# Seven of eight 128-row tiles of a second layer's input transposed by VectorE in 32x32 blocks and by SBUF-to-SBUF transfers

## Chip, cores, metric

One Trainium2 chip, one of its cores. The metric is the device time of one launch in microseconds (us); lower is better.

## What is computed

A two-layer decoder trunk over 1024 prompt tokens and 32 sample tokens, with 1024 features, all float32. Layer 0 mixes tokens with a gated short convolution, layer 1 with a gated linear recurrence (HGRN2). Both layers have this shape:

```
h = rms_norm(x, norm_pre[i])
proj = h @ w_in[i]                      # 1024 x 4096
o = mixer(proj)                         # convolution or recurrence, gated by silu(z)
x = x + rms_norm(o @ w_out[i], norm_post[i])
```

The change touches the place between the layers: layer 0's last line, and layer 1's first (`x` after layer 0, normalised by its rows, and brought from rows of tokens to columns of tokens, since the projection contracts over features and needs features on the partitions).

## The kernel before

Everything is written by hand, engine by engine, with counted semaphores; an engine runs its instructions in the order in which they are written. The token rows of the prompt are cut into eight tiles of 128 (below "row 0" to "row 7"; index `i`, `CK` = 8). Matrix products are made with a high and a low part of each float32 operand, as three products.

The stage between the layers runs like this, for each row i:

- **TensorE** makes the output product of the row (`products`, 48 matmuls of 128x512, L819) into two PSUM banks, 2(i mod 3) and the next. Rows 0 to 2 are done together, first; rows 3 to 7 follow one by one, and row i starts only when VectorE has read row i-3 out of those banks (event `t1`). The transposes of a finished row stand within the products of a later row (`TURN`): `turn_rows(i)` is eight 128x128 transposes against the identity (L836) into banks 6 and 7.
- **ScalarE** squares the product for the norm (`squares_y`, L1390), takes the root (L1397), squares the new x (L1390 again), takes its root, makes the high part of the transposed previous row (`turned_hi`, L1423), and starts the squares of the next row.
- **VectorE** scales the product by `norm_post` (L2082), adds the residual (L2092, event `x1`), scales the previous row's transpose by `norm_pre` out of PSUM (`turned`, L2107), normalises its own row (L2140, event `xn`), and makes the low part of the previous row's transpose (`turned_lo`, L2113).
- **SP** issues the transfers: the new x of the row to DRAM (L494), and the load of x for row i+3 (`load_x`, L456), which waits for `xn` of row i and for the store to have landed, since both use the same one of three buffers.

The normalised row is in `o_n[i % 2]` (its first use in row i is as scratch of ScalarE's squares), its transpose in `o_tr[i % 2]`. The 32 sample tokens have a path of their own; their transpose lies in `o_tr[1]` until its low half is made (event `lo` of `Q_DVE[0]`, L2072), after row 0's low half.

After row 7's product TensorE goes on to layer 1: groups of 24 matmuls (L674), one for a third c of the tokens (352 columns) and a projection i. Their order is `FIRST`, and row 7's transposes stand behind the second group:

```
FIRST = ((0, 0), (0, 1), (1, 0), (1, 1), (0, 2), (1, 2), (2, 0), (2, 1), (2, 2))
pe.wait_ge(V_TR.sem, V_TR.at((2, 5, 7)[c], "lo"))       # first projection alone
```

So group (0, 0) needs rows 0 to 2 transposed and split, group (0, 1) rows up to 5, group (0, 2) all of them. Group (1, 0) writes the bank of group (0, 0), which ScalarE empties (L1438) behind the high half of row 6. In row 6 (`CK - 2`) ScalarE and VectorE also split two weight tiles for layer 1 (L1184, L1715).

Of the kernel before, what the change touches and what calls it, by code (L numbers as in the profile page):

```python
# [41 lines left out]
F_FLOOR = 2.061153622438558e-09  # L42
QSCALE = float(P) ** -0.5
B4, B8 = 4, 8
NG = 4
GR = NSAMP // NG
LEVELS = (8, 16, 32, 64)
# [45 lines left out]
def build(nc, x_prompt, x_sample, state_conv, state_hgrn, norm_pre, w_in, conv_w, lb_logits, onorm,  # L93
          w_out, norm_post, y_prompt, y_sample, conv_p, conv_s, hgrn_p, hgrn_s):
    ctx = ExitStack()
    with ctx:
# [3 lines left out]
        def sem(name):  # L100
            return ctx.enter_context(nc.semaphore(name))
# [210 lines left out]
        A_P2 = Events(sem("out2_act"), ["s0", "s1", "sd1"])  # L312
        V_P2 = Events(sem("out2_dve"), ["t0", "ms", "t1", "rs", "x"])
        first_half_x = sem("first_half_x")
        Q_PE = [Events(sem("sample_pe"), ["y", "n1", "n2", "tr"]), Events(sem("sample2_pe"), ["y", "n1"])]
        Q_ACT = [Events(sem("sample_act"), ["sq", "sd", "sq2", "sd2", "hi"]), Events(sem("sample2_act"), ["sq", "sd"])]
        Q_DVE = [Events(sem("sample_dve"), ["t", "rs", "x", "rs2", "xn", "g", "lo"]),
# [42 lines left out]
        def wsrc(w, col):  # L360
            return w[:, bass.ds(col, P)].rearrange("(k p) c -> p k c", p=P)
# [34 lines left out]
        def _(sp):  # L396
# [81 lines left out]
            sp.wait_ge(cout, 32)  # L478
            sp.dma_start(o_g, norm_post[0:1, :].broadcast_to([P, D])).then_inc(g_in, 16)

            QC, FC, VC, ZC = 0, D, 2 * D, 3 * D
            for i in range(CK):
                if i == 0:
                    for first in range(3):
                        load_x(first)
                    sp.wait_ge(Q_PE[0].sem, Q_PE[0].at(0, "y"))
                    load_w(NW2, wsrc(w_in[1], VC), 0, None)
                    load_w(NW2 + 1, wsrc(w_in[1], QC), 1, None)
                    sp.wait_ge(Q_DVE[0].sem, Q_DVE[0].at(0, "x"))
                    for q in range(4):  # L490
                        cols, own = quarter(q)
                        sp.dma_start(x1_dram[NP:T, cols], smp_x[0][own, :]).then_inc(smp_kept, 16)
                sp.wait_ge(V_PO.sem, V_PO.at(i, "x1"))
                sp.dma_start(x1_dram[i * P:i * P + rows_of(i), :], o_x[i % 3][0:rows_of(i), :]).then_inc(stored[i % 3], 16)  # L494
                if i + 3 < CK:
                    load_x(i + 3)
            load_w(NW2 + 2, wsrc(w_in[1], FC), 0, None)
            with sp.Fori(1, KT) as j:
                for t, col in enumerate((QC, ZC - P, VC, FC)):
# [131 lines left out]
        def _(pe):  # L631
# [193 lines left out]
            def turn_rows(i):  # L825

                r = rows_of(i)
                pe.wait_ge(V_PO.sem, V_PO.at(i, "xn"))
                if i == 0:
                    pe.wait_ge(Q_DVE[0].sem, Q_DVE[0].at(0, "g"))  # L830
                if i:
                    pe.wait_ge(V_TR.sem, V_TR.at(i - 1, "gb"))
                for half, name in enumerate(("ta", "tb")):
                    for k in range(4):
                        kk = half * 4 + k
                        mm = nc.tensor.transpose(bank[6 + half][:, k * P:k * P + r],  # L836
                                                 o_n[i % 2][0:r, kk * P:(kk + 1) * P], ident[0:r, 0:r])
                    mm.then_inc(P_TR.now(name), 1)
# [35 lines left out]
            for cc in range(2):  # L874
                mm = nc.tensor.transpose(bank[7][:, (1 + cc) * P:(2 + cc) * P], smp_n[:, cc * P:(cc + 1) * P], ident[:, :])
            mm.then_inc(Q_PE[0].now("tr"), 1)
            TURN = {(3, 3): 0, (4, 3): 1, (4, 7): 2, (5, 7): 3, (6, 3): 4, (6, 7): 5, (7, 7): 6}
            for i in range(3, CK):
                pe.wait_ge(V_PO.sem, V_PO.at(i - 3, "t1"))
                for k in range(KT):  # L880
                    b = 2 * (i % 3)
                    mm = products(k, ((b, 0), (b + 1, 1)), wout_tile(reg_b, k), o0, i, k == 0, k == KT - 1)
                    if k == KT - 1:
                        mm.then_inc(y_done, 1)
                    elif i == CK - 1 and k < 2:
                        mm.then_inc(w_used, 1)
                    if (i, k) in TURN:
                        turn_rows(TURN[i, k])


            h1, o1 = planes(reg_a), planes(reg_b)
# [284 lines left out]
        def _(act):  # L1176
# [233 lines left out]
            def squares_y(i):  # L1410

                r = rows_of(i)
                if i >= 2:
                    act.wait_ge(P_TR.sem, P_TR.at(i - 2, "tb"))
                act.wait_ge(y_done, i + 1)
                for half in range(2):
                    square(bank[2 * (i % 3) + half][0:r, :], o_n[i % 2][:, half * HALF:(half + 1) * HALF], A_PO,
# [290 lines left out]
        def _(dve):  # L1708
# [386 lines left out]
            def turned(i):  # L2095

                r = rows_of(i)
                dst = o_tr[i % 2].rearrange("p (k t) -> p k t", k=KT)
                if i >= 2:
                    dve.wait_ge(A_TR.sem, A_TR.at(i - 2, "hi"))  # L2100
                    dve.wait_ge(V_TR.sem, V_TR.at(i - 2, "lo"))
                for half, (name, g_name) in enumerate((("ta", "ga"), ("tb", "gb"))):
                    dve.wait_ge(P_TR.sem, P_TR.at(i, name))
                    src = bank[6 + half][:, :].rearrange("p (k t) -> p k t", k=4)[:, :, 0:r]
                    first = PRE + KT + 4 * half
                    g = cst[:, first:first + 4].unsqueeze(2).broadcast_to([P, 4, r])
# [15 lines left out]
            for i in range(CK):  # L2122
# [9 lines left out]
                    sample_next("xn")  # L2132
                elif i == 1:
                    sample_next("g")
                if i:
                    turned(i - 1)
                dve.wait_ge(A_PO.sem, A_PO.at(i, "sd2"))
                V.reciprocal(col(i, "rs2", r), col(i, "sd2", r)).then_inc(V_PO.now("rs2"), 1)
                dve.wait_ge(V_PO.sem, V_PO.at(i, "rs2"))
                V.tensor_scalar(o_n[i % 2][0:r, :], o_x[i % 3][0:r, :], col(i, "rs2", r), None,  # L2140
                                ALU.mult).then_inc(V_PO.now("xn"), 1)
                if i:
                    turned_lo(i - 1)
                if i == 1:
                    sample_next("lo")
# [373 lines left out]
```

## Time and profile before

| | |
|---|---|
| time, median of 3 runs | 1034.37 us (1034.27 to 1034.69) |
| span of the profiled execution | 1032.7 us |
| TensorE busy | 1025.7 us, 99% of the span |
| VectorE busy | 705.2 us, 68% |
| ScalarE busy | 426.3 us, 41% |
| matmuls of layer 0's output product (L819, rows 0 to 7) | about 353 to 453 us |
| row 7's transposes on TensorE | from 460.9 us |

The span runs from the first to the last instruction; the time of a launch is 1.7 us more. Busy times are sums over the whole kernel, so what counts for the change is the stage from about 385 to 475 us from the span's start.

### The profile page before, as it was taken

The numbers are of one execution on the slowest core, as the hardware profiler recorded it, in microseconds if no ns is written. First come the engines' busy times: TensorE is split into PE (matmuls) and PEld (weight loads), VectorE is DVE, ScalarE is ACT, GpSimd is POOL, SyncE is SP. The second block draws the span as 40 slices with busy tenths as digits, with TensorE's granted clock in tenths as the row PEclk, the third lists the DMA queues.
The fourth block names the chain that finished last, engine by engine and source line by source line (L and its number), as shares of the span: only waits on it lengthen the run. The fifth ranks groups of instructions, "written<-read, shape, count | busy, mean of one in ns | idle before, by whom it ended". The sixth has DMA issues, their size and how long they took to land.

```text
span 1032.7 us, 20543 instructions
## 1 busy us (share of the span) xinstructions
PE 1025.7 (99%) x7979; PEld 977.3 (95%) x7979; DVE 705.2 (68%) x1274; ACT 426.3 (41%) x860; POOL 18.3 (2%) x45
## 2 busy tenths in 40 slices
PE   9999999999999999999999999999999999999998
PEld 8999999999999978899999999999999999997886
DVE  6899677677776926762857768485776848586355
ACT  7444333333333624443345443443534344383222
POOL 2000000000000000000000000000000000000000
PEclk9999999999999999999999999999999999999999
DMA  8003121112112253321212211221221122143064
GB/s 253 22 22 82 42 82 41 41 53 69 41 41 63 101 173 114 120 82 42 58 46 64 63 35 49 63 59 45 61 61 43 41 63 61 60 150 110 25 241 169
DMA packets 95552, 78.75 MB, mean 76 GB/s; under 512 B 2965, under 2 KB 86886, under 8 KB 95510
## 3 DMA queue, kind: packets, MB, share of 16 engines
q1 hardware_dynamic: 77622, 69.19, 21.5%
q10 hardware_dynamic: 17888, 8.98, 3.0%
q8 instruction: 29, 0.48, 0.2%
q14 instruction: 13, 0.11, 0.0%
HBM read 64.72 MB, written 13.44 MB: 76 GB/s over the span
## 4 chain that ended last, share of the span: by engine, by line
PE 97%; DVE 2%; DMA 1%; ACT 0%; SPq 0%; issue 0%; DVEq 0%
PE bank L674 36%; PE bank L731 28%; PE bank L819 14%; PE bank L699 4%; PE bank L1069 4%; PE bank L913 2%; PE bank L1025 1%; PE bank L1018 1%; PE bank L1027 1%; PE bank L929 1%; PE bank L801 1%; PE bank L921 1%; PE bank L836 1%; PE bank L1013 1%; PE bank L977 1%; PE bank L908 1%
## 5 line engine op out<-in xcount | busy, mean ns | idle before, releaser
L674 PE MATMUL bank<-reg_a,wsplit 128*128 128x352 f32 x2304 | 381.5, 324 | 0.0
L674 PEld LDWEIGHTS bank<-reg_a,wsplit 128*128 128x128 f32 x2304 | 368.6, 188 | 1.1
L731 PE MATMUL bank<-reg_a,wsplit 128*128 128x264 f32 x1344 | 165.7, 284 | 0.0
L731 PEld LDWEIGHTS bank<-reg_a,wsplit 128*128 128x128 f32 x1344 | 164.1, 188 | 0.2 <-DVE arena L1902 0.2
L731 PE MATMUL bank<-reg_b,w_ring 128*128 128x264 f32 x1008 | 124.6, 284 | 0.0
L731 PEld LDWEIGHTS bank<-reg_b,w_ring 128*128 128x128 f32 x1008 | 123.3, 188 | 0.0
L819 PE MATMUL bank<-reg_b,reg_a 128*128 128x512 f32 x288 | 69.3, 396 | 0.0
L819 PEld LDWEIGHTS bank<-reg_b,reg_a 128*128 128x128 f32 x288 | 53.7, 188 | 12.7 <-issue 0.4
L1930 DVE TENSOR_TENSOR arena<-arena,bank 128x264 f32<-128x264 f32 x84 | 34.8, 427 | 34.2 <-PE bank L731 33.1
L1290 ACT ACTIVATE arena<-bank 128x264 f32<-128x264 f32 x84 | 32.3, 390 | 55.1 <-PE bank L731 50.4
L1268 ACT ACTIVATE w_ring<-wraw 128x512 fp32r<-128x512 f32 x42 | 26.1, 632 | 69.1 <-PE bank L731 69.0
L2413 DVE COPY arena<-bank 128x128 f32<-128x128 f32 x8 | 2.3, 292 | 66.2 <-PE bank L1018 66.2
L1268 ACT ACTIVATE wsplit<-wraw 128x512 fp32r<-128x512 f32 x42 | 25.0, 628 | 49.1 <-DMA wraw<-in_w_in 36.1
L1715 DVE TENSOR_TENSOR wsplit<-wraw,wsplit 128x1024 fp32r<-128x1024 f32 x32 | 39.1, 1222 | 4.7 <-ACT wsplit L1184 4.7
L819 PE MATMUL bank<-reg_a,reg_b 128*128 128x512 f32 x168 | 39.8, 394 | 0.0
L2441 DVE SCALAR_TENSOR_TENSOR arena<-arena,bank 128x352 f32<-128x352 f32 x45 | 23.3, 518 | 24.0 <-ACT arena L1434 18.6
L819 PEld LDWEIGHTS bank<-reg_a,reg_b 128*128 128x128 f32 x168 | 31.6, 188 | 7.5
L1184 ACT ACTIVATE wsplit<-wraw 128x1024 fp32r<-128x1024 f32 x32 | 33.7, 1054 | 0.7 <-PE bank L819 0.7
L1440 ACT ACTIVATE arena<-bank 128x352 f32<-128x352 f32 x24 | 11.2, 465 | 55.1 <-PE bank L674 55.0
L2082 DVE TENSOR_TENSOR arena<-bank,arena 128x512 f32<-128x512 f32 x24 | 16.3, 686 | 25.1 <-ACT arena L1390 25.0
L1878 DVE TENSOR_TENSOR w_ring<-wraw,w_ring 128x512 fp32r<-128x512 f32 x42 | 28.8, 690 | 6.5 <-ACT w_ring L1268 6.5
L1492 ACT ACTIVATE kv_stacked<-v_stacked,bmask 96x128 fp32r<-96x128 f32 x64 | 19.6, 391 | 31.6 <-DVE arena L2349 31.6
(299 smaller groups left out, 1499.5 us busy)
## 6 DMA issues: line engine op xcount, KB each, us to landing
wraw<-in_w_in SPq DMA_DIRECT2D x64, 512.0 KB, 4.1
first_x<-in_x_prompt SPq DMA_DIRECT2D x8, 512.0 KB, 7.4
wraw<-in_w_out SPq DMA_DIRECT2D x8, 512.0 KB, 4.0
w_out_raw<-in_w_out SPq DMA_DIRECT2D x8, 512.0 KB, 5.1
arena<-in_w_out SPq DMA_DIRECT2D x8, 512.0 KB, 4.7
arena<-in_x_prompt SPq DMA_DIRECT2D x8, 512.0 KB, 3.3
x_scratch<-arena SPq DMA_DIRECT2D x8, 512.0 KB, 2.6
arena<-in_state_hgrn ACTq DMA_DIRECT2D x8, 512.0 KB, 3.8
```

What stands on the lines that cost most here:

```text
L674: mm = nc.tensor.matmul(bank[b][:, 0:CH], w[wi][:, k, :], rhs[hi], start=(k == 0 and i == 0), stop=(k == KT - 1 and i == 2))
L699: mm = nc.tensor.matmul(bank[b][:, 0:QT], w[wi][:, k, :], src[hi][:, k % KH, cols], start=(k == 0 and i == 0), stop=(k == KT - 1 and i == 2))
L731: mm = nc.tensor.matmul(bank[banks[q]][:, 0:QT], w[wi][:, k, :], B_OP[name][hi][:, k, q * QT:(q + 1) * QT], start=(start and k == 0 and i ...
L819: mm = nc.tensor.matmul(bank[b][0:r, :], src[side][:, k, i * P:i * P + r], w[wi][:, half * HALF:(half + 1) * HALF], start=(start and side ...
L1069: mm = nc.tensor.matmul(bank[PART_BANK[n]][:, :], o1[side][:, k, i * P:(i + 1) * P], wout_tile(reg_a, k)[wi][:, half * HALF:(half + 1) * H ...
L1184: A(wsplit[:, s, 0] if dst is None else dst, wraw[:, s], ACT.Copy).then_inc(w_hi, 1)
L1268: A(w_block(name)[0], A_RAW[name], ACT.Copy).then_inc(W_HI.now(name), 1)
L1290: A(dst[:, q * QT:(q + 1) * QT], bank[banks[q]][:, 0:QT], ACT.Copy).then_inc(C_ACT.now(f"{what}{s}{q}"), 1)
L1715: V.tensor_tensor(d, wraw[:, s], h.bitcast(F32), ALU.subtract).then_inc(w_lo, 1)
L1878: V.tensor_tensor(lo, A_RAW[name], hi.bitcast(F32), ALU.subtract).then_inc(W_LO.now(name), 1)
L1930: V.tensor_tensor(dst[:, cols], src[:, cols], bank[banks[q]][:, 0:QT], ALU.add).then_inc(C_DVE.now(f"{what}{s}{q}"), 1)
L2441: V.scalar_tensor_tensor(buf[:, cols], buf[:, cols], QSCALE if kind == "q" else 1.0, bank[c][:, 0:CH], ALU.mult, ALU.mult).then_inc(bank_f ...
```

## The change

Rows 0 to 6 are no longer transposed by TensorE. VectorE transposes the 32x32 blocks of the normalised row in place (`V.transpose`), and SP then moves each block row into its place with 16 transfers of 32 partitions, 8 feature tiles and 32 elements (32 KB each, runs of 128 bytes). VectorE then scales the transpose by `norm_pre` in one instruction in SBUF. The old buffers' waits become waits for the transfers. Row 7 and the sample tokens are transposed as before. `turned(i - 1)` has also moved on VectorE from ahead of row i's normalisation to behind it.

```diff
+            def move_row(i):
+
+                sp.wait_ge(row_turned, i + 1)
+                if i == 1:
+                    sp.wait_ge(Q_DVE[0].sem, Q_DVE[0].at(0, "lo"))
+                elif i >= 2:
+                    sp.wait_ge(V_TR.sem, V_TR.at(i - 2, "lo"))
+                blocks = o_n[i % 2].rearrange("p (k d t) -> p d k t", k=KT, d=NQD)
+                rows = o_tr[i % 2].rearrange("p (k b t) -> p b k t", k=KT, b=NQD)
+                for d in range(NQD):
+                    for b in range(NQD):
+                        sp.dma_start(rows[d * BLK:(d + 1) * BLK, b],
+                                     blocks[b * BLK:(b + 1) * BLK, d]).then_inc(row_moved[i % 2], 16)
...
                 if i + 3 < CK:
                     load_x(i + 3)
+                if i < LAST_ROW:
+                    move_row(i)
...
-            TURN = {(3, 3): 0, (4, 3): 1, (4, 7): 2, (5, 7): 3, (6, 3): 4, (6, 7): 5, (7, 7): 6}
...
-                    if (i, k) in TURN:
-                        turn_rows(TURN[i, k])
...
                 if i >= 2:
-                    act.wait_ge(P_TR.sem, P_TR.at(i - 2, "tb"))
+                    act.wait_ge(row_moved[i % 2], i // 2 * MOVED)
...
+                if i < LAST_ROW:
+                    dve.wait_ge(row_moved[i % 2], (i // 2 + 1) * MOVED)
+                    g = cst[:, PRE + KT:PRE + 2 * KT].unsqueeze(2).broadcast_to([P, KT, r])
+                    V.tensor_tensor(dst, dst, g, ALU.mult).then_inc(*V_TR.many("ga", "gb"))
+                    return
...
-                if i:
-                    turned(i - 1)
                 dve.wait_ge(A_PO.sem, A_PO.at(i, "sd2"))
                 V.reciprocal(col(i, "rs2", r), col(i, "sd2", r)).then_inc(V_PO.now("rs2"), 1)
                 dve.wait_ge(V_PO.sem, V_PO.at(i, "rs2"))
                 V.tensor_scalar(o_n[i % 2][0:r, :], o_x[i % 3][0:r, :], col(i, "rs2", r), None,
                                 ALU.mult).then_inc(V_PO.now("xn"), 1)
+                if i < LAST_ROW:
+                    dve.wait_ge(V_PO.sem, V_PO.at(i, "xn"))
+                    V.transpose(o_n[i % 2], o_n[i % 2]).then_inc(row_turned, 1)
                 if i:
+                    turned(i - 1)
                     turned_lo(i - 1)
```

On VectorE, one row of the loop (row 2) stood like this before, from the scaling of the product to the low part of row 1 (L2082 scales the product, L2107 the transpose, L2140 normalises, L2113 makes the low part):

```order
L2082 TENSOR_TENSOR arena<-bank,arena 128x512
L2085 RECIPROCAL small<-small 128x1
L2092 SCALAR_TENSOR_TENSOR arena<-arena,small 128x1024
L2107 TENSOR_TENSOR arena<-bank,cst 128x512 x2
L2138 RECIPROCAL small<-small 128x1
L2140 TENSOR_SCALAR arena<-arena,small 128x1024
L2113 TENSOR_TENSOR reg_a<-arena,reg_a 128x8x128
```

And so after the change, where the lines are some 16 to 20 higher (L2098 for L2082, L2118 for the scaling of the transpose, L2158 for L2140, L2133 for L2113, and L2162 is new):

```order
L2098 TENSOR_TENSOR arena<-bank,arena 128x512
L2101 RECIPROCAL small<-small 128x1
L2108 SCALAR_TENSOR_TENSOR arena<-arena,small 128x1024
L2156 RECIPROCAL small<-small 128x1
L2158 TENSOR_SCALAR arena<-arena,small 128x1024
L2162 STREAM_TRANSPOSE arena<-arena 128x1024
L2118 TENSOR_TENSOR arena<-arena,cst 128x1024
L2133 TENSOR_TENSOR reg_a<-arena,reg_a 128x8x128
```

The scaling of the previous row's transpose has moved from between the residual and the normalisation to behind the new block transpose, directly ahead of the low part.

On SP's queue, rows 0 to 2 are now written like this (L514 is the store that was L494, L462 the load that was L456, L498 the new transfers; `arena` holds `o_x`, `o_n` and `o_tr` alike):

```order
L514 DMA x_scratch<-arena 128x1024
L462 DMA arena<-in_x_prompt 128x1024
L498 DMA arena<-arena 32x8x32 x16
L514 DMA x_scratch<-arena 128x1024
L462 DMA arena<-in_x_prompt 128x1024
L498 DMA arena<-arena 32x8x32 x16
```

The 16 transfers of a row stand behind that row's store and load and ahead of the next row's; rows 5 and 6 have no load. Before, the same queue held the L494 and L456 rows alone.

## Rows read from the trace of the kernel before

**Rows 1.** The page: span, TensorE's line, and its granted clock in tenths.
```profile
span 1032.7 us, 20543 instructions
...
PEclk9999999999999999999999999999999999999999
```

**Rows 2.** Chain that ended last, 380 to 475 us: start, duration, piece.
```profile
391.57 5.58 PE bank L819 x24
397.15 0.87 PE bank L836 x8
398.02 11.17 PE bank L819 x48
...
453.52 7.69 PE bank L674 x48
```

**Rows 3.** Waits, 382 to 475 us: total, times, longest.
```profile
DVE arena L2107 <- PE bank L836: 16.3, 6, 5.7
```

**Rows 4.** Timeline, ScalarE and VectorE, one row of tokens: start, duration, instruction, idle before.
```profile
409.67 1.29 DVE L2107 TENSOR_TENSOR arena<-bank,cst 128x512 f32<-128x512 f32 x2 [5.41 <-PE bank L836]
...
410.99 1.06 ACT L1423 ACTIVATE reg_a<-arena 128x1024 fp32r<-128x1024 f32 x1 [5.22 <-DVE arena L2107]
...
414.69 1.28 DVE L2092 SCALAR_TENSOR_TENSOR arena<-arena,small 128x1024 f32<-128x1024 f32 x1
...
416.01 1.06 ACT L1390 ACTIVATE arena<-arena 128x1024 f32<-128x1024 f32 x1 [1.69 <-DVE arena L2092]
...
417.72 0.75 DVE L2140 TENSOR_SCALAR arena<-arena,small 128x1024 f32<-128x1024 f32 x1
```

**Rows 5.** VectorE groups by shape, whole kernel: busy us, mean ns.
```profile
L2206 DVE COPY_PREDICATED arena<-mask_within,bank 64x512 f32<-64x512 uint8 x14 | 10.4, 741 | 0.1
...
L2113 DVE TENSOR_TENSOR reg_a<-arena,reg_a 128x1024 fp32r<-128x1024 f32 x8 | 9.8, 1226 | 2.2 <-ACT reg_a L1423 2.1
...
L2140 DVE TENSOR_SCALAR arena<-arena,small 128x1024 f32<-128x1024 f32 x8 | 6.0, 754 | 0.3
```

**Rows 6.** Timeline of SP's DMA queue, 340 to 500 us.
```profile
361.77 0.43 SPq L472 DMA_DIRECT2D arena<-in_x_sample  x1
362.24 0.42 SPq L473 DMA_DIRECT2D arena<-in_norm_post  x1
...
365.49 0.76 SPq L475 DMA_DIRECT2D out<-arena  x1
...
389.23 0.34 SPq L494 DMA_DIRECT2D x_scratch<-arena  x1
392.33 0.37 SPq L456 DMA_DIRECT2D arena<-in_x_prompt  x1
```

**Rows 7.** DMA view: queues, then issues with median us to landing.
```profile
q1 hardware_dynamic: 77622, 69.19, 21.5%
q10 hardware_dynamic: 17888, 8.98, 3.0%
...
x_scratch<-arena SPq DMA_DIRECT2D x4, 32.0 KB, 1.7
```

**Rows 8.** Timeline, VectorE: first row's normalised tile; the sample tokens' lower half.
```profile
390.94 0.76 DVE L2140 TENSOR_SCALAR arena<-arena,small 128x1024 f32<-128x1024 f32 x1
...
401.19 0.42 DVE L2072 TENSOR_TENSOR reg_a<-arena,reg_a 128x256 fp32r<-128x256 f32 x1
```

**Rows 9.** Timeline, end of the stage, as rows 4.
```profile
442.95 1.28 DVE L2092 SCALAR_TENSOR_TENSOR arena<-arena,small 128x1024 f32<-128x1024 f32 x1
...
445.27 1.04 ACT L1390 ACTIVATE arena<-arena 128x1024 f32<-128x1024 f32 x1
...
458.03 0.75 DVE L2140 TENSOR_SCALAR arena<-arena,small 128x1024 f32<-128x1024 f32 x1
458.65 0.45 ACT L1438 ACTIVATE arena<-bank 128x352 f32<-128x352 f32 x1
...
461.83 8.41 PE L674 MATMUL bank<-reg_a,wsplit 128*128 128x352 f32 x51
```

More of the change, by code:

```diff
@@ L44 @@
 B4, B8 = 4, 8
+BLK = 32
+NQD = P // BLK
+MOVED = NQD * NQD * 16
+LAST_ROW = CK - 1
 NG = 4
@@ L314, in build @@
         first_half_x = sem("first_half_x")
+        row_turned = sem("rows_turned_in_blocks")
+        row_moved = [sem(f"row_blocks_moved{i}") for i in range(2)]
         Q_PE = [Events(sem("sample_pe"), ["y", "n1", "n2", "tr"]), Events(sem("sample2_pe"), ["y", "n1"])]
@@ L828, in turn_rows @@
                 pe.wait_ge(V_PO.sem, V_PO.at(i, "xn"))
-                if i == 0:
-                    pe.wait_ge(Q_DVE[0].sem, Q_DVE[0].at(0, "g"))
-                if i:
-                    pe.wait_ge(V_TR.sem, V_TR.at(i - 1, "gb"))
+                pe.wait_ge(Q_DVE[0].sem, Q_DVE[0].at(0, "g"))
                 for half, name in enumerate(("ta", "tb")):
@@ L2098, in turned @@
                 dst = o_tr[i % 2].rearrange("p (k t) -> p k t", k=KT)
-                if i >= 2:
-                    dve.wait_ge(A_TR.sem, A_TR.at(i - 2, "hi"))
-                    dve.wait_ge(V_TR.sem, V_TR.at(i - 2, "lo"))
+                if i < LAST_ROW:
[3 more added lines that the diff above has]
+                    return
+                dve.wait_ge(A_TR.sem, A_TR.at(i - 2, "hi"))
+                dve.wait_ge(V_TR.sem, V_TR.at(i - 2, "lo"))
                 for half, (name, g_name) in enumerate((("ta", "ga"), ("tb", "gb"))):
-                    dve.wait_ge(P_TR.sem, P_TR.at(i, name))
+                    dve.wait_ge(P_TR.sem, P_TR.at(0, name))
                     src = bank[6 + half][:, :].rearrange("p (k t) -> p k t", k=4)[:, :, 0:r]
@@ L2134, in _ @@
                     sample_next("g")
-                if i:
-                    turned(i - 1)
                 dve.wait_ge(A_PO.sem, A_PO.at(i, "sd2"))
```

## The prediction, made before the run

> **What bounds the kernel now.** The chain that ended last comes first: between 380 and 475 us it is TensorE alone, piece behind piece [rows 2]. A row's 48 matmuls take 11.17 us there, and the eight transposes of a row stand in it with 0.87 us. The clock is full in every slice [rows 1]. So seven transposes less are worth 7 x 0.87 = 6.1 us, the most that this change can give, as long as nobody else makes TensorE wait. The next view is who else is near. The waits show VectorE waiting 16.3 us for the transposes [rows 3]; TensorE has no wait of note. That wait goes, and something else takes its place, so the loop over VectorE, ScalarE and now SP must be costed, not only TensorE. The timeline of one row of tokens gives its pieces [rows 4]. The loop has a deadline: group (0, 1), which needs rows to 5; row 7's transposes, which need row 7 normalised; and group (1, 0), which needs ScalarE past row 6's high half. It starts at 461.83 us now [rows 9], and I take the change in that start as the change in the kernel's time, since behind it the chain is TensorE without gaps.
>
> **TensorE's side.** Row 3 starts at 391.57 us; five rows of 11.17 us end at 447.4 us, where group (0, 0) could start instead of at 453.52 us [rows 2]. That is the 6.1 us.
>
> **The loop over VectorE and ScalarE.** Call T(i) the end of row i's block transpose, M(i) the landing of its last transfer. Behind T(i), VectorE must scale row i-1's transpose, wait for ScalarE's high part, make the low part, do all of row i+1 to its normalisation, and transpose again. Before, the same pieces run from 409.67 us (scaling begins) to 417.72 + 0.75 = 418.47 us (row normalised): 8.80 us without a wait for TensorE [rows 4]. The squares and the root of the new x, from 416.01 us to just ahead of 417.72, are in it in full, so that nothing more is exposed when the scaling no longer lies beside them. The scaling becomes one SBUF instruction, 1.29 us to about 1.23 us (the 128x1024 tensor-tensor form) [rows 4, 5]: 8.74 us. The block transpose is new, and the trace shows none. Bounds: 0.75 us, the fastest 128x1024 row, and 1.48 us, twice a predicated copy of 512 elements [rows 5]. I take 1.23 us, as for other one-element-a-cycle forms of the width. So C = 10.0 us a row, of 11.17 us that TensorE needs. The slack is 1.2 us a row, if the transfers of a row land within C.
>
> **The transfers.** Sixteen issues a row on SP. The nearest issue is one of 32 partitions: 0.43 us, and 0.47 us from start to start (361.77 to 362.24) [rows 6]: 16 x 0.465 = 7.4 us. The bounds are 0.34 us (the 128-row store) and 0.76 us (the three-level store L475) [rows 6]. The last one lands 1.7 us after its issue if it is like the 32 KB store [rows 7]: 15 x 0.465 + 1.7 = 8.7 us from the row's first issue. Each of the 16 DMA engines gets 256 runs of 128 bytes a row. The ACT queue's packets took 3.0% of 16 x 1032.7 us for 17,888, that is 27.7 ns for 502 bytes; SP's took 45.8 ns for 891 bytes [rows 7]. A line through both says 4 ns and 0.046 ns a byte, 10 ns for 128 bytes; so 256 of them take between 2.7 and 7.1 us, less than their issue, but behind the 512 KB load just ahead of them in the queue. The upper value adds about 1.5 us. I take 9.6 us from first issue to landing.
>
> SP's own round also matters, and every transfer in it counts: the 16 issues (7.4), then the next row's store, whose landing the next load waits for (389.23 to 392.33 is 3.1 us from store to load), then the load's issue (0.37) [rows 6]. Before, this wait lay behind other things. Now it stands between two rows' transfers: 10.9 us, and 11.2 us with some of the queueing. Queued behind these issues on SP are also the store and load of the next rows, which have slack, and the weight load behind row 7's store.
>
> The Trainium skill bears on the packet price: DMA: Bandwidth & Descriptors, "Why small descriptors are slow (HBM only)", says that SBUF-to-SBUF transfers do not pay the small-run penalty, while its "Specifications" ask for 512 bytes for line rate. No row here has runs of 128 bytes. By the one the sum is bound by the issue, by the other it is the slow rival below.
>
> **The sum, row by row.** T(0) = 390.94 + 0.76 + 1.23 = 392.9 us [rows 8]; the first issue follows, S(0) = 392.95, M(0) = 402.55. Row 1's transfers write `o_tr[1]`, so they wait for the sample's low part, which stands behind row 0's scaling, high and low parts: 1.23 + 1.06 + 1.23 + 0.42 = 4.0 us behind M(0) [rows 4, 5, 8]. That is a wait of its own, S(1) = 406.55, M(1) = 416.15. Then S(2), S(3), S(4) = 417.75, 428.95, 440.15 (11.2 apart), M(2), M(3), M(4) = 427.35, 438.55, 449.75. The transposes: T(2) = M(0) + 10.0 + 0.4 (sample) = 412.95, and T(i) = M(i-2) + 10.0 for the next ones, since each M comes 1 to 3 us behind the T of the row after it: T(5) = 448.55. T(6) = 449.75 + 10.0 + 0.9 = 460.65 us. The 0.9 us is row 6's two weight splits on ScalarE: the square comes 1.04 us behind the residual there (end 444.23, start 445.27) [rows 9], in other rows 0.04 us (415.97, 416.01) [rows 4].
>
> From T(6) on: row 5's scaling, high and low parts, 3.6 us (464.25: group (0, 1) may start); the weight split on VectorE 1.23 us; row 7 from its scaling to its residual 2.7 us (what remains of the 8.80 us without the other pieces) and on to its normalisation 2.5 us (415.97 to 418.47) (470.7: row 7's transposes on TensorE); M(6) = T(6) + 9.6 = 470.3 is just ahead; row 6's scaling 1.23 us, high part 1.06 us, bank emptied by ScalarE 0.45 us [rows 4, 9]. Group (1, 0) starts at about 473.5 us instead of 461.83: **+11.7 us**. On the median this gives 1034.4 + 11.7 = 1046.1 us; the profiled execution's span lies 1.7 us below the median before, and I expect 1044.4 us for it. TensorE saves 6.1 us and then stands for some 18 us: before (0, 0), (0, 1), row 7's transposes and (1, 0).
>
> **The rivals.**
>
> *Cheap transfers.* If issues come 0.34 us apart, transfers land 6.8 us after the first issue and SP's round is 8.9 us, under C. Then VectorE's loop alone decides: M(0) = 399.75, T(2) = 410.15, T(6) = 451.5, (1, 0) at 464.3: +2.5 us, 1037 us. With a block transpose of 0.75 us it is 2.9 us less, 1034 us. For it: such issues are in the trace. Against it: none of them has partial partitions.
>
> *The saving shows.* The other sign: VectorE's loop keeps ahead of TensorE. With a 0.75 us transpose and transfers that always land within the loop, T(1) = 398.45, T(6) = 447.25, (1, 0) at 460.05: -1.8 us, 1032.6 us; the 6.1 us (1028.3) need 4 us more somewhere in a chain that has no idle time left. It decides below 0.27 us an issue, which no row shows.
>
> *Slow transfers.* At 0.76 us an issue, the landing takes 14.0 us and SP's round 15.6 us: M(4) = 471.75, T(6) = 482.6, M(6) = 496.7, (1, 0) at 499.5: +37.7 us, 1072 us. If instead the packets are slow, twice 27.7 ns, a row takes 14.2 + 3.0 us of the DMA engines, and the same steps end at about 1090 us. For it: the L475 row, and that no row has such short runs. Against it: L475 has 8 partitions in its slowest dimension, unlike these.
>
> *The clock falls.* TensorE's granted clock is full now, with no long idle stretch in its work [rows 1, 2]. In the forecast it stands 7 and 6 us before its two groups. At 1.2 GHz group (0, 0) (3.85 us, half of the 7.69 us of two groups [rows 2]) ends before the low part of row 5 anyway, and (0, 1) before row 7 is normalised or 1 to 2 us later; if the next two run slow too, that is +3.9 us each: 1046 to 1054 us. The Trainium skill, TensorE: Matmul & The Clock Gate, "HAM oscillation", says that idle stretches of this size bring the half clock back; no stretch of this trace tests it.
>
> **How the numbers follow.** Chances: forecast (1038 to 1056 us at full clock) 0.50, the clock as well 0.12, slow transfers 0.22, cheap transfers 0.11, the saving 0.05. The predicted time is 1046 us, the forecast's own range 1038 to 1056. The 8-in-10 range, 1035 to 1072 us, leaves out the saving, some of the cheap case and half of the slow one. A difference of 0.2% (2.1 us) is about what a measurement of this kernel can tell from no change: faster (below 1032.3) 0.05, within it 0.07 (the lower part of the cheap case), slower 0.88.
>
> **What the profile after would show.** If right: 112 transfers of 32 KB, issued about 0.46 us apart; VectorE's scaling of the transposes (L2118) waiting for DMA, not for TensorE, from row 0 on, by 1 to 3 us and more in row 0; a block transpose of about 1.2 us; group (0, 1) waiting for the low part, row 7's transposes for the normalised row, and (1, 0) for ScalarE; matmuls of rows 3 to 7 without gaps. The prediction is wrong if the issues or the runs cost something else, if the block transpose is far from 1.2 us, or if work that I hold to be serial overlaps, the high and low parts above all.

## The result, and the profile after

The change makes the kernel slower: 1063.54 us in the median of 4 runs (1063.24 to 1064.85), against 1034.36 us for the kernel before on the same chip. The ratio is 1.0284, with a 95% interval of 1.0271 to 1.0297. That is +29.2 us where +11.7 us was forecast. The direction held, and the time lies inside the 8-in-10 range (1035 to 1072 us), but outside the forecast's own range (1038 to 1056 us); the size was off by 17.5 us. One of the ten launches of the kernel with one transfer a row, below, took 1105.38 us at a granted clock of 0.85 and is left out of its ratio; without it that kernel's median is 1036.88 us in place of 1037.0. The page of the profiled execution, span and granted clock in tenths:

```profile
span 1061.4 us, 20544 instructions
...
PEclk9999999999999999968999999999999999999999
```

The span has grown by 28.7 us, and two slices have a lowered clock, 0.6 and 0.8 in the mean (before, none: [rows 1]). The timeline of TensorE shows where the time lies (start, duration, instruction, idle time before it and what ended it):

```profile
425.82 3.06 PE L841 MATMUL bank<-wsplit,reg_a 128*128 128x512 f32 x12 [0.99 <-DVE arena L2098]
...
440.90 4.62 PE L841 MATMUL bank<-wsplit,reg_a 128*128 128x512 f32 x12 [3.62 <-DVE arena L2098]
...
470.70 6.21 PE L696 MATMUL bank<-reg_a,wsplit 128*128 128x352 f32 x24 [16.80 <-DVE wsplit L1731]
478.10 4.08 PE L696 MATMUL bank<-reg_a,wsplit 128*128 128x352 f32 x24 [1.20 <-issue]
484.35 1.09 PE L855 MATMUL bank<-ident,arena 128*128 128x128 f32 x8 [2.17 <-DVE arena L2158]
488.80 36.45 PE L696 MATMUL bank<-reg_a,wsplit 128*128 128x352 f32 x216 [3.36 <-ACT arena L1454]
```

Group (1, 0) is the last row. It starts at 488.80 us instead of 461.83 us [rows 9]: 27.0 us later. The 216 matmuls from there on take 36.45 us; in the kernel before they take 34.81 us, and in the kernels of the experiments whose clock was whole there 34.80 or 34.81 us. These 1.6 us are the other part: 27.0 + 1.6 = 28.6 of 28.7 us. TensorE waits for VectorE in rows 6 and 7 already, 0.99 and 3.62 us (L2098, scaling the product), and longest, 16.80 us, ahead of group (0, 0), for a weight's low part that stands in VectorE's row 6.

VectorE's own waits, in the view of waits (total, times, longest):

```profile
DVE arena L2118 <- DMA arena<-arena: 26.5, 7, 6.0
```

The 16.3 us that VectorE waited for transposes [rows 3] have become 26.5 us of waiting for transfers. The block transpose itself is as forecast; its line in the trace:

```profile
L2162 DVE STREAM_TRANSPOSE arena<-arena x7: 1245/1245/1248, 391.5 to 472.1; 128x1024 f32<-128x1024 f32 x7
```

What makes the transfers late shows in SP's queue (start, time of the issues, instruction):

```profile
409.13 10.39 SPq L498 DMA_DIRECT2D arena<-arena  x16
419.57 0.60 SPq L514 DMA_DIRECT2D x_scratch<-arena  x1
422.51 0.34 SPq L462 DMA_DIRECT2D arena<-in_x_prompt  x1
422.95 11.29 SPq L498 DMA_DIRECT2D arena<-arena  x16
434.28 0.60 SPq L514 DMA_DIRECT2D x_scratch<-arena  x1
```

and one by one in the chain from 405 to 420 us:

```profile
411.73 0.61 SPq L498
412.34 0.04 issue
412.38 0.61 SPq L498
...
419.57 2.88 DMA x_scratch<-arena
```

An issue takes 0.61 us and the next starts 0.65 us after it, where 0.465 us was forecast. The round from one row's first issue to the next row's, 409.13 to 422.95, is 13.8 us: 10.4 for the issues, 2.9 from store to load (the landing of the store), 0.4 for the load. The DMA engines have time left meanwhile; the view of windows, with TensorE's clock, the share of the DMA engines and GB/s as the last three columns:

```profile
411.00:419.00 8.00, 8.00 (x36) 6.46 (x35) 2.88 (x4) 1.45 (x3) 0.00 (x0) 1.00 0.31 51
...
450.00:470.00 20.00, 3.90 (x17) 2.82 (x15) 12.25 (x18) 8.61 (x18) 0.00 (x0) 0.71 0.44 105
```

They are busy 0.31 of the time in a stretch in which the row's transfers alone run. In the second window TensorE idles ahead of group (0, 0), and the granted clock is 0.71 in the mean; from 461 to 470 us it is 0.50, the lower of its two levels.

### The profile page after: what moved, and what is told of

Its sections match the earlier page's. It is cut to its first block, busy times and chain, and to the rows that moved or that the text cites. A ratio compares the mean times of both kernels' runs of the same rounds, so it can differ in the third digit from the quotient of the medians.

```text
span 1061.4 us, 20544 instructions
## 1 busy us (share of the span) xinstructions
PE 1025.9 (97%) x7923; PEld 975.6 (92%) x7923; DVE 713.4 (67%) x1274; ACT 425.7 (40%) x860; POOL 18.2 (2%) x45
## 4 chain that ended last, share of the span: by engine, by line
PE 87%; SPq 7%; DVE 3%; DMA 1%; issue 1%; ACT 0%; POOL 0%; POOLq 0%; DVEq 0%
PE bank L696 34%; PE bank L753 27%; PE bank L841 7%; SPq L498 6%; PE bank L721 4%; PE bank L1085 4%; PE bank L929 2%; PE bank L1034 1%; PE bank L1041 1%; PE bank L1043 1%; DMA x_scratch<-arena 1%; PE bank L945 1%; PE bank L823 1%; PE bank L937 1%; PE bank L1029 1%
## 5 line engine op out<-in xcount | busy, mean ns | idle before, releaser
L696 PE MATMUL bank<-reg_a,wsplit 128*128 128x352 f32 x2304 | 385.5, 326 | 21.3 <-DVE wsplit L1731 16.8
L2445 DVE TENSOR_REDUCE small<-arena 128x4 f32<-128x512 f32 x16 | 10.2, 681 | 31.4 <-ACT arena L1621 31.4
```

Source lines behind the costliest of these rows:

```text
L696: mm = nc.tensor.matmul(bank[b][:, 0:CH], w[wi][:, k, :], rhs[hi], start=(k == 0 and i == 0), stop=(k == KT - 1 and i == 2))
```

## The experiments

Each kernel ran on one chip with the kernel before beside it, and its ratio is to that. Edits are to the changed kernel where nothing else is said.

**Runs of 256 bytes.** Theory A: the price of a transfer is that of its runs. Theory B: it is the issue's, whatever it moves. The same bytes go in half the runs; the elements land in other places than the transposition needs.

```diff
-                blocks = o_n[i % 2].rearrange("p (k d t) -> p d k t", k=KT, d=NQD)
-                rows = o_tr[i % 2].rearrange("p (k b t) -> p b k t", k=KT, b=NQD)
+                blocks = o_n[i % 2].rearrange("p (k d t) -> p d k t", k=KT // 2, d=NQD)
+                rows = o_tr[i % 2].rearrange("p (k b t) -> p b k t", k=KT // 2, b=NQD)
```

> The changed kernel with each of the 16 transfers of a row cut into 128 runs of 256 bytes in place of 256 runs of 128 bytes (same bytes, same 16 transfers; the elements land in another order, so the data is not the transpose). Theory A, an issue is held back by the descriptors of the one before it, about 2.6 ns a run (0.655 us for 256): from start to start 0.35 to 0.47 us, a row's issues 5.6 to 7.5 us, the kernel 1042 to 1049 us. Theory B, the price is one of the instruction and its shape: 0.65 us from start to start as in the changed kernel, 1063 us.

Measured: 1063.08 us, ratio 1.0275 (1.0255 to 1.0296), with rounds of 13.7, 15.4 and 13.7 us (13.8, 14.7 and 13.8 in the changed kernel; the 15.4 us hold two issues of 1.3 and 1.6 us). The issues of a row without such long ones take 10.25 us for 10.39. Theory A falls.

**One transfer a row.** It copies the row whole, so the transposition is left out.

```diff
-MOVED = NQD * NQD * 16
+MOVED = 16
...
-                for d in range(NQD):
-                    for b in range(NQD):
-                        sp.dma_start(rows[d * BLK:(d + 1) * BLK, b],
-                                     blocks[b * BLK:(b + 1) * BLK, d]).then_inc(row_moved[i % 2], 16)
+                sp.dma_start(o_tr[i % 2], o_n[i % 2]).then_inc(row_moved[i % 2], 16)
```

> The changed kernel with one transfer of 128x1024 a row in place of the 16 (no block changes its partitions, so the data is not the transpose). All waits stand. Theory: what is left is the loop over VectorE and ScalarE, 10.0 us a row and serial, which alone is too slow to let TensorE's saving show: T(6) about 451 us, group (1, 0) at 464, 1036 to 1038 us, no faster than before. Rival: without slow transfers the 6.1 us of transposes come out: 1028 to 1030 us.

Measured: 1037.0 us, ratio 1.0023 (1.0013 to 1.0033). TensorE's timeline:

```profile
447.15 4.01 PE L693 MATMUL bank<-reg_a,wsplit 128*128 128x352 f32 x24
452.70 4.11 PE L693 MATMUL bank<-reg_a,wsplit 128*128 128x352 f32 x24 [1.54 <-issue]
458.95 1.09 PE L852 MATMUL bank<-ident,arena 128*128 128x128 f32 x8 [2.14 <-DVE arena L2155]
461.61 37.45 PE L693 MATMUL bank<-reg_a,wsplit 128*128 128x352 f32 x216 [1.57 <-ACT arena L1451]
```

So 15 issues a row less take 26.5 us off. Group (0, 0) starts at 447.15 us, some 6 us earlier than before [rows 2]: here TensorE's saving is to be seen. By group (1, 0), at 461.61 us, all but 0.2 us of it is gone, in waits for VectorE and ScalarE, whose loop takes 9.9 us a row. The 216 matmuls then take 2.6 us more than at the whole clock, as much as the kernel loses.

**The load behind the transfers.** `load_x(i + 3)` goes behind `move_row(i)`, so that SP no longer waits for the store's landing between two rows' transfers.

```diff
-                if i + 3 < CK:
-                    load_x(i + 3)
                 if i < LAST_ROW:
                     move_row(i)
+                if i + 3 < CK:
+                    load_x(i + 3)
```

> The changed kernel with the load of x for row i+3 issued behind row i's transfers, not ahead of them. Theory: SP's round was 13.8 us, of which some 2.9 us is the wait for the store's landing ahead of that load; the round falls to about 11.4 us and the rows' transfers follow each other sooner: group (1, 0) at about 480.5 us, 1055 us. Rival: the DMA engines or the VectorE loop set the round, and the wait for the store lay beside them: 1062 to 1064 us.

Measured: 1060.99 us, ratio 1.0258 (1.024 to 1.0275): a miss. The first issues of rows 1 to 3 are at 409.80, 421.41 and 434.67 us, 11.6 to 13.3 us apart. The wait is gone, and the issues are left: 10.4 to 12.0 us for 16, since in most rows one or two issues take 1.2 to 1.6 us. The transfers alone are above VectorE's 9.9 us a row, whatever else is in the queue.

**Runs of 1024 bytes, transposition kept.** VectorE normalises into another order of columns and reads the transpose by other patterns, so that each transfer has 32 runs of 1 KB.

```diff
-                blocks = o_n[i % 2].rearrange("p (k d t) -> p d k t", k=KT, d=NQD)
-                rows = o_tr[i % 2].rearrange("p (k b t) -> p b k t", k=KT, b=NQD)
+                blocks = o_n[i % 2].rearrange("p (d c) -> p d c", d=NQD)
+                rows = o_tr[i % 2].rearrange("p (b c) -> p b c", b=NQD)
```

> The changed kernel with the normalised row written with its features in the order 32-block, tile, and the transpose kept by row block, so that each of the 16 transfers of a row moves 32 runs of 1 KB; everything else as in the change, and the output right. Theory A (price by runs): issues 0.42 to 0.47 us apart, SP's round 10.5 to 11.2 us, 1044 to 1049 us, which is what the prediction's sum gave. Theory B (price of the instruction): 1062 to 1066 us. Against both: VectorE's or ScalarE's instructions may slow down on the new access patterns, 0.5 us each a row, 3 to 6 us in all.

Measured: 1061.43 us, ratio 1.0262 (1.0245 to 1.028), 0.6 us below theory B's range and far from theory A's. In the timeline of SP's queue a row of transfers:

```profile
408.76 10.01 SPq L498 DMA_DIRECT2D arena<-arena  x16
```

An eighth of the runs changes the price of an issue from 0.61 to 0.59 us.

**Eight transfers of 64 partitions a row** (a copy, the transposition is left out).

```diff
-                for d in range(NQD):
+                for half in range(2):
                     for b in range(NQD):
-                        sp.dma_start(rows[d * BLK:(d + 1) * BLK, b],
-                                     blocks[b * BLK:(b + 1) * BLK, d]).then_inc(row_moved[i % 2], 16)
+                        at = slice(half * 2 * BLK, (half + 1) * 2 * BLK)
+                        sp.dma_start(rows[at, b], blocks[at, b]).then_inc(row_moved[i % 2], 16)
```

> The changed kernel with 8 transfers a row of 64 partitions x 8 x 32 in place of 16 of 32 partitions (same bytes, same 256-run-per-32-partitions shape; the blocks don't change their partitions, so the data is not the transpose). Theory B, the price is one of an issue, about 0.65 us whatever it moves: a row's issues 5.2 us, landing 6.5 us after the first, under the VectorE loop, so the kernel falls nearly to that of one transfer a row: 1037 to 1040 us. Rival: the price goes with the partitions or bytes of a transfer, then it is 1.3 us an issue and the time stays at 1061 to 1064 us.

Measured: 1038.46 us, ratio 1.0036 (1.0023 to 1.0049). SP's queue, two rows:

```profile
404.78 5.35 SPq L499 DMA_DIRECT2D arena<-arena  x8
...
432.79 5.44 SPq L499 DMA_DIRECT2D arena<-arena  x8
```

That is 0.67 us each, with twice the bytes and partitions in each; the two rows between them took 6.4 and 5.9 us, with single issues of 1.7 and 1.1 us. Theory B holds: the number of transfers counts.

**By way of DRAM, transposition kept.** Four writes of 32 partitions to DRAM place the block columns, and one read of 128 partitions brings the row back. VectorE and ScalarE use the order of columns of the kernel with runs of 1024 bytes.

```diff
+                blocks = o_n[i % 2].rearrange("p (d c) -> p d c", d=NQD)
+                rows = turn_dram[i].rearrange("(d j) (b c) -> b j d c", d=NQD, b=NQD)
+                for b in range(NQD):
+                    sp.dma_start(rows[b], blocks[b * BLK:(b + 1) * BLK]).then_inc(row_out[i % 2], 16)
...
+                sp.wait_ge(row_out[i % 2], (i // 2 + 1) * NQD * 16)
+                sp.dma_start(o_tr[i % 2], turn_dram[i]).then_inc(row_moved[i % 2], 16)
```

> The changed kernel with the blocks sent by 4 transfers to DRAM (32 partitions each, runs of 1 KB, placed as the transpose) and fetched by one transfer of 128x1024: 5 issues a row in place of 16, but two landings in series; output right. Theory B: 4 x 0.43 + 1.7 to land + 0.35 + 3.4 is about 7.3 us from first issue to landing, under the 9.9 us of the VectorE loop; group (1, 0) at about 462.4 us, and TensorE's clock, which fell there with one transfer a row too, costs 2.6 us: 1037 to 1039 us. Rival: the second landing in series and DRAM traffic give back what the issues save: above 1045 us.

Measured: 1043.87 us, ratio 1.0081 (1.0066 to 1.0097), between the two expectations and above the theory's: a miss. SP's queue, one round:

```profile
413.87 1.94 SPq L495 DMA_DIRECT2D turn_scratch<-arena  x4
418.97 0.34 SPq L501 DMA_DIRECT2D arena<-turn_scratch  x1
419.35 0.43 SPq L516 DMA_DIRECT2D x_scratch<-arena  x1
424.76 0.33 SPq L464 DMA_DIRECT2D arena<-in_x_prompt  x1
```

The five issues cost 2.3 us, but the writes land 3.4 us after an issue (I had 1.7 us, from 32 KB), and the store's landing, behind the read in the queue, holds the load for 5.4 us. From row 1 to row 4 the rounds are 10.9, 11.3 and 12.5 us, above VectorE's loop.

**Rows 0 to 3 by DRAM, rows 4 to 6 by TensorE.** The edit is `LAST_ROW = 4` in the kernel by way of DRAM, with TensorE's transposes of the other rows where they were before.

```diff
-LAST_ROW = CK - 1
+LAST_ROW = 4
...
+            TURN = {(6, 3): 4, (6, 7): 5, (7, 7): 6}
```

> As the kernel that goes by DRAM, but only rows 0 to 3 by blocks and transfers; rows 4 to 6 by TensorE at the places where they stood before the change; output right. Theory: the deadline is at the end of the stage, where VectorE has idle time only if TensorE's transposes stay, so the early rows' 4 x 0.87 = 3.5 us come out: 1030.5 to 1032.5 us, faster than before. Rival: any delay of the VectorE loop in the early rows is carried to the end: 1034 to 1040 us.

Measured: 1041.92 us, ratio 1.0064 (1.005 to 1.0078): a miss. What the rival described took place, but the time lies 1.9 us above its range too. TensorE's timeline:

```profile
433.66 1.58 PE L859 MATMUL bank<-ident,arena 128*128 128x128 f32 x8 [2.74 <-DVE arena L2182]
...
445.49 1.97 PE L859 MATMUL bank<-ident,arena 128*128 128x128 f32 x8 [3.57 <-DVE arena L2182]
```

The turned rows make VectorE late, and TensorE waits for rows 4 and 5 to be normalised. Around these waits its clock falls too: row 5's eight transposes take 1.97 us at a granted clock of 0.50, for 1.04 us at the whole clock.

**The clock kept.** Matmuls of 512 columns on idle operands fill TensorE's waits ahead of group (0, 0), group (0, 1) and group (1, 0) (60, 10 and 9) and ahead of row 7's transposes (5).

```diff
+            def fill(n):
+                for _ in range(n):
+                    nc.tensor.matmul(bank[4][:, :], wout_tile(reg_b, 4)[0][:, 0:P],
+                                     wout_tile(reg_b, 5)[0][:, 0:HALF], start=True, stop=True)
...
+                if n == 0:
+                    pe.wait_ge(V_PO.sem, V_PO.at(5, "t1"))
+                fill({0: 60, 1: 10, 2: 9}.get(n, 0))
```

> The changed kernel with idle TensorE filled: 60 matmuls of 128x512 whose result nobody reads ahead of group (0, 0), 10 ahead of (0, 1), 5 ahead of row 7's transposes, 9 ahead of (1, 0). Theory: the low clock in those stretches is hidden behind the waits except in the first groups from (1, 0) on, where the trace shows 216 matmuls in 36.45 us against 34.81 before: 1.6 us, so 1061.5 to 1062.5 us, and group (1, 0) still at about 488.8. Rival: the low clock also holds back the chain that ends in (1, 0): below 1060 us.

Measured: 1062.88 us, ratio 1.0273 (1.0258 to 1.0289), an interval that overlaps the changed kernel's (1.0271 to 1.0297): the medians alone don't tell the two apart, the traces do. TensorE's timeline from group (1, 0):

```profile
489.53 34.80 PE L696 MATMUL bank<-reg_a,wsplit 128*128 128x352 f32 x216 [1.18 <-ACT arena L1463]
```

The clock is whole, and the 216 matmuls are 1.6 us shorter. Of it 0.7 us are lost again, since the group starts later (489.53 us for 488.80): the last transfers of row 6 land 0.7 us later in this execution, so VectorE scales the row at 486.72 us for 485.99.

**The copy kernel with its clock kept.** The same in the kernel with one transfer a row, with 5 matmuls ahead of group (0, 1), 7 ahead of row 7's transposes and 5 ahead of group (1, 0) (the expectation below names the last two numbers the other way round).

```diff
+                fill({1: 5, 2: 5}.get(n, 0))
                 pe.wait_ge(w_lo, NW2 + i + 1)
...
                 if n == 1:
+                    fill(7)
                     turn_rows(CK - 1)
```

> The kernel with one transfer a row (which leaves out the transposition, its output is wrong by that) took 1037.0 us, with 216 matmuls from group (1, 0) on in 37.45 us instead of 34.81, at a lower granted clock. Here TensorE multiplies idle operands in its three idle stretches ahead of group (0, 1), of row 7's transposes and of group (1, 0) (5, 5 and 7 matmuls of 512 columns into a free bank). Theory: all that this kernel loses against before is the clock: 1034.4 us, full clock throughout, 216 matmuls in 34.8 us; up to 0.7 us more if the added matmuls end late. Rival (the loss is the later start): 1036.5 to 1037.5 us at a full clock.

Measured: 1034.55 us, ratio 0.9999 (0.999 to 1.0009). TensorE's timeline:

```profile
461.75 34.80 PE L693 MATMUL bank<-reg_a,wsplit 128*128 128x352 f32 x216 [0.41 <-ACT arena L1458]
```

Group (1, 0) starts where it did in the unfilled one (461.61 us), and the 2.5 us are gone. With nearly free transfers the change is worth nothing, and its waits, of 1.5 to 2.1 us each, cost 2.6 us by the clock alone.

**Two queues, transposition kept.** GpSimd, idle in this stage, issues 6 of a row's 16 transfers.

```diff
-                for d in range(NQD):
-                    for b in range(NQD):
+                for n in range(10):
+                    d, b = divmod(n, NQD)
...
+            for i in range(LAST_ROW):
+                pool.wait_ge(row_turned, i + 1)
...
+                for n in range(10, 16):
+                    d, b = divmod(n, NQD)
+                    pool.dma_start(rows[d * BLK:(d + 1) * BLK, b],
+                                   blocks[b * BLK:(b + 1) * BLK, d]).then_inc(row_moved_p[i % 2], 16)
```

> The changed kernel with six of a row's sixteen transfers issued by GpSimd, which is idle in this stage, and ten by SP. Theory (what costs is the serial issue on one queue): SP's ten take 6.6 us, the last one lands about 8.5 us after the first issue if GpSimd issues its six in less than 6.5 us, SP's round is about 10.5 us, first issues at about 416, 426.5 and 437 us for rows 2 to 4, group (1, 0) starts at about 468 us, and the time is 1040 to 1044 us. Rival 1 (issues of both queues share one limit, behind the queues): the last landing stays at 12.4 us, 1060 to 1064 us. Rival 2 (GpSimd issues at 1.5 us or more each): it becomes the later one, 9 us and more of issue, 1048 to 1063 us.

Measured: 1041.66 us, ratio 1.0068 (1.0052 to 1.0084), as the theory said. The queues of SP and of GpSimd in the timeline, the same row of tokens:

```profile
405.81 6.49 SPq L498 DMA_DIRECT2D arena<-arena  x10
406.33 3.44 POOL L649 DMA_DIRECT2D arena<-arena  x6 [9.52 <-DVE reg_a L2102]
```

Both issue at once, SP at its 0.65 us, GpSimd at 0.57 us. The limit is each queue's: beside GpSimd's issues, SP's are no slower. The same transfers with the same bytes are 21.9 us faster.

**Rows 0 to 2 by DRAM.** The edit is again to the kernel by way of DRAM: rows 3 to 6 go by TensorE, as before, and the load stands behind the writes.

```diff
-LAST_ROW = CK - 1
+LAST_ROW = 3
...
-                if i + 3 < CK:
-                    load_x(i + 3)
                 if i < LAST_ROW:
                     move_row(i)
+                if i + 3 < CK:
+                    load_x(i + 3)
...
+            TURN = {(5, 7): 3, (6, 3): 4, (6, 7): 5, (7, 7): 6}
```

> Rows 0 to 2 alone are turned in blocks by VectorE, with four writes to DRAM and one read back; rows 3 to 6 are transposed by TensorE as before, and the load of x stands behind the writes, so that the read is not behind it. Theory (a turned row pays only where VectorE's loop has time left before TensorE asks for the next transposed row): the third row's landing comes about 2 us earlier than with rows 0 to 3, row 3 is normalised at about 420 us and TensorE asks for it at 423.7 us, row 4 at 429 against 431, row 5 at about 437.9 against 437.8. TensorE saves three times 0.87 us and keeps its clock: 1031.8 us, 2.6 us faster than before (ratio 0.9975). Rival (the delay of the turned rows is carried to row 4 or 5, as in the run with rows 0 to 3): TensorE waits 1 to 3 us there, 1033 to 1036 us.

Measured: 1032.07 us, ratio 0.9976 (0.9966 to 0.9985), 2.4 us faster than before. TensorE's timeline has no wait in the stage:

```profile
437.59 1.04 PE L859 MATMUL bank<-ident,arena 128*128 128x128 f32 x8
...
458.99 34.81 PE L698 MATMUL bank<-reg_a,wsplit 128*128 128x352 f32 x216
```

**Rows 0 to 3 by DRAM, later transposes.** Against the kernel with rows 0 to 3 by DRAM two things change: the load stands behind the writes (as in the diff above), and rows 4 and 5 are transposed half a row later.

```diff
-            TURN = {(6, 3): 4, (6, 7): 5, (7, 7): 6}
+            TURN = {(6, 7): 4, (7, 3): 5, (7, 7): 6}
```

> As the run that turned rows 0 to 3 by VectorE and DRAM and took 1041.9 us, with the load of x behind the writes, and with TensorE's transposes of rows 4, 5 and 6 one place later in its products (rows 4 and 5 in the second half of row 6 and the first half of row 7). Theory: the 6.3 us that TensorE waited for the normalised rows 4 and 5 there go; VectorE has row 5 normalised at about 440 us and TensorE asks at 442.6 us; TensorE saves four times 0.87 us: 1031 to 1032 us. Rival: the weights' low parts and row 7's chain on VectorE, which come behind, are late instead, since VectorE now waits for the later transposes: TensorE waits ahead of group (0, 0) or of row 7's transposes, 1034 to 1039 us.

Measured: 1031.04 us, ratio 0.9965 (0.9953 to 0.9978), 3.45 us faster than before, which is four times 0.87 us. How much of the 10.9 us against the earlier kernel with rows 0 to 3 by DRAM is the load's place and how much the later transposes, no run separates. TensorE's timeline:

```profile
435.89 1.03 PE L859 MATMUL bank<-ident,arena 128*128 128x128 f32 x8
...
442.37 1.03 PE L859 MATMUL bank<-ident,arena 128*128 128x128 f32 x8
...
458.18 34.81 PE L698 MATMUL bank<-reg_a,wsplit 128*128 128x352 f32 x216
```

## Why the prediction was right in kind and too small

**Right.** The path is the forecast's in the main: SP's issues make the scaling of the transposes wait for DMA in each row, that makes VectorE late, and TensorE stands ahead of the same groups. Not forecast were TensorE's waits within rows 6 and 7 (the prediction expected the matmuls of rows 3 to 7 without gaps). The block transpose took 1.245 us (1.23), and row 1's transfers start 4.0 us behind M(0) (405.1 to 409.13 us). VectorE's loop without late transfers is 9.9 us (10.0), in the kernel with one transfer. The runs of 128 bytes are not the bound: the line through the two queues said 10 ns a run, and the window from 411 to 419 us gives nearly the same: 0.31 of 8 us is 2.5 us of each engine, for 8 / 0.65 = 12.3 transfers of 16 runs an engine, 12.6 ns a run.

**The step that failed** is the price of an issue in "The transfers": "The nearest issue is one of 32 partitions: 0.43 us, and 0.47 us from start to start". It is 0.65 us. That row's likeness was its 32 partitions; it read from DRAM. The kernels with 128 and 32 runs in place of 256 show that the pattern hardly counts, and the eight transfers that neither partitions nor bytes do. From start to start, issues from SBUF to SBUF took 0.63 to 0.67 us on SP's queue in every kernel that had more than one a row, apart from single long ones of 1.1 to 1.7 us; a row's four writes to DRAM, in the kernel by way of DRAM, took 0.44 to 0.49 us each. With 0.65 us in place of 0.465 and nothing else changed, the prediction's own sum gives (an estimate) 12.4 us from first issue to landing, rounds of 14.2 us, M(4) = 464.2, T(6) = 475.1 and M(6) = 487.5 us, and starts group (1, 0) at 490.2 us: +28.4 us. The bounds that I gave, 0.34 and 0.76 us, held it; the value chosen between them did not.

This one term enters at four places. SP's queue and VectorE's timeline have the last ones:

```profile
451.47 10.40 SPq L498 DMA_DIRECT2D arena<-arena  x16
...
463.28 1.22 DVE L2118 TENSOR_TENSOR arena<-arena,cst 128x1024 f32<-128x1024 f32 x1 [3.83 <-DMA arena<-arena]
...
472.13 1.25 DVE L2162 STREAM_TRANSPOSE arena<-arena 128x1024 f32<-128x1024 f32 x1
...
485.99 1.23 DVE L2118 TENSOR_TENSOR arena<-arena,cst 128x1024 f32<-128x1024 f32 x1 [1.70 <-DMA arena<-arena]
```

Redone with what the trace shows:

- M(0) is 405.1 instead of 402.55 us, since the landing took 12.4 us instead of 9.6: 11.0 from the first issue's start to the last one's end, one of them of 1.1 us, and 1.3 from there to the landing. So S(1) is 2.6 us later.
- Three rounds of 13.8, 14.7 and 13.8 us instead of 11.2 bring S(4) to 451.47 instead of 440.15 us: 8.7 us more, of which 0.9 us is one issue of 1.5 us in row 2.
- The landing of row 4 took 11.8 us: 2.2 us more. M(4) is 463.3 us for 449.75, T(6) 473.4 for 460.65.
- M(6) comes 12.5 us behind T(6). The prediction had it "just ahead" of VectorE; now it is the last, and group (1, 0) follows it by 2.9 us, at 488.8 for 473.5 us.

That is 15.3 of the 17.5 us missing. 1.6 us are the clock. Of the last 0.6 us, 0.5 is that the span grew by 28.7 and the median by 29.2 us. The two other terms of the round were right: 2.9 us from store to load (3.1) and 0.44 us for the load (0.37). The 0.9 us for row 6's weight splits was not there, which takes 0.8 us off T(6): in the kernel with one transfer row 6's loop is 9.99 us, like the others. In the changed kernel ScalarE makes the two splits from 467.75 to 469.74 us, while VectorE makes the residual, and the square starts 0.15 us behind the residual's end (469.50), not 1.04 us: they lay in ScalarE's slack.

**The rivals.** *Slow transfers* named the mechanism that took place, at 0.76 us an issue; my 0.22 for it stood against 0.50 for the middle value, and what I held against it, the 8 partitions of L475's slowest dimension, was no evidence on an issue from SBUF to SBUF. *Cheap transfers* gave 1037 us, and the kernel with one transfer took 1037.0. This agreement is partly chance: its group (1, 0) starts at 461.6 us, not at 464.3, and the clock takes 2.6 us. *The saving shows* does not come true even there. VectorE's loop is 1.3 us a row shorter than TensorE's 11.17, but starts late and is lengthened at its end by row 7's serial chain. *The clock falls* took place, to 0.71 of full speed in the mean from 450 to 470 us. Of it 1.6 us were left in the time; the kernel with its clock kept shows it, and the half clock in group (0, 0), 6.21 us for 24 matmuls, lay in VectorE's shadow as forecast.

The Trainium skill, DMA: Bandwidth & Descriptors, "Issuing engines are not separate DMA queues", says that a second issuing engine saves only the time of initiating, and calls this "usually small relative to the DMA itself". The first half agrees with the two queues: moving 6 issues of 16 saved 3.9 us of a row's 10.4; the second doesn't hold here, where issuing a row takes 10.4 us and the last landing comes 1.3 us behind the last issue's end. Its section "Why small descriptors are slow (HBM only)", weighed ahead, was right as far as the time of this kernel goes: from 128 to 1024 bytes a run it changed by 2.1 us of 1063.5. But a kernel that its issues bound can't test it fully, and the traces show that short runs do cost the DMA engines more: in stretches with a row's transfers alone, at 51 or 52 GB/s, they were busy 0.31 of the time with 128 bytes a run, 0.25 with 256 and 0.20 with 1024.

**Left open.** Why issues from SBUF to SBUF take 0.6 us each in a row, when the single one of 128 rows took 0.47 to 0.55 us, and what makes one or two issues in some rows take 1.1 to 1.7 us, no run shows. Writes to DRAM can be dear too: in the two kernels with the load behind the writes, row 1's four writes, issued close behind a load and a store, took 3.5 and 3.7 us, those of the other rows 1.8 to 2.1 us.

## What to carry to other kernels

Count a row's transfers before its bytes: a queue that issues one after another has a rate of its own, and it bounds the loop when the number of transfers times that price, with each landing that the queue waits for between them, comes near the loop's time. Where an operation's price has bounds that give another verdict or twice the loss, and the row chosen differs in where the data come from, give both ends like chances. Work that frees the bound engine is worth its full size only as long as the engine that takes it over has waits to fill: here three or four rows of seven, by DRAM, gave their 0.87 us each, and all seven gave none, even in the kernel with one transfer a row and its clock kept, though the waits of VectorE summed over the stage [rows 3] seemed to have room.

## What the hardware did that I had not expected

- Issues on one hardware queue cost alike for 32 KB in 256, 128 or 32 runs and for 64 KB on 64 partitions (0.63 to 0.67 us from start to start, single long ones apart); GpSimd's cost 0.57 us, no more than SP's, and ran beside them without slowing them.
- In the kernel with one transfer a row TensorE's granted clock fell in the third of three waits of only 1.5 to 2.1 us, the first from 451.2 us and the last to 461.6 us, with full work between them: 216 matmuls took 37.45 us against 34.80 with these waits filled. It was full up to 460 us, within the third wait, 0.80 in the mean from 460 to 461 us, 0.50 from there to 467 us, and full again from 468 us. In the changed kernel, whose waits were longer, up to 16.8 us, they took 36.45 us, less than there.
- A write of 128 KB from SBUF to DRAM landed 3.4 us after its issue in the median, twice the 1.7 us of 32 KB [rows 7], when the 512 KB load stood directly ahead of the row's four writes, and 2.5 and 2.2 us in the two kernels that issue the load behind them. So a part of the 3.4 us comes from what stands ahead in the queue, not from the size.
